# Value products with the weights as the moving operand: two heads on different column halves, output already turned

## The reference

```
p = softmax(q k^T * scale + bias)           # A; B: p1 - lam * p2; C: exp(log weights); D: with a sink
o = einsum('hqk,khd->qhd', p, v)            # 256 queries x 64 per head, causal
branch = o.reshape(256, 256) @ w_br[b]      # 256 x 1024, times sigmoid(h @ w_gate[b]), summed over b
```

## Time and profile before

| | |
|---|---|
| median of 3 runs | 709.2 us (707.84 to 709.97) |
| the profiled execution | 708.31 us, of which the span is 706.5 us |
| TensorE busy | 681.2 us, 96% of the span |
| VectorE, ScalarE busy | 246.4 us, 192.7 us |
| DMA | 243.57 MB, mean 345 GB/s |
| granted TensorE clock | 0.992 of 2.4 GHz over the span |

### The profile page before, as it was taken

How to read it: one execution, slowest core, us unless ns; L and a number is a source line. 1 busy time by engine, 2 the same in 40 slices (tenths; PEclk the granted TensorE clock), 3 DMA queues, 4 the chain that set the end, 5 groups by cost and what they waited for, 6 DMA issues and landing times.

```text
span 706.5 us, 9936 instructions
## 1 busy us (share of the span) xinstructions
PE 681.2 (96%) x4047; PEld 398.2 (56%) x4047; DVE 246.4 (35%) x528; ACT 192.7 (27%) x305; POOL 5.2 (1%) x9
## 2 busy tenths in 40 slices
PE   9999999999999999999999999999989898998995
PEld 6999887777777864344344344344344343453433
DVE  7563566667677772121121121121121010210212
ACT  6443565588565421110110010010010010100113
POOL 0000000000000000000000000000000000000000
PEclk9999999999999999999999999999999999999998
DMA  8897741383659959999999999999999999999994
GB/s 311 290 274 232 280 138 54 106 298 119 179 160 384 397 250 376 418 428 426 425 428 427 424 428 426 429 427 426 429 429 428 429 429 424 429 423 428 417 397 169
DMA packets 47053, 243.57 MB, mean 345 GB/s; under 512 B 10352, under 2 KB 13608, under 8 KB 33704
## 3 DMA queue, kind: packets, MB, share of 16 engines
q1 hardware_dynamic: 46568, 241.45, 85.7%
q0 software_dynamic: 448, 1.59, 0.7%
HBM read 241.96 MB, written 1.07 MB: 344 GB/s over the span
## 4 chain that ended last, share of the span: by engine, by line
PE 73%; DMA 17%; DVE 5%; ACT 2%; issue 2%; POOLq 0%; SPq 0%; DVEq 0%; ACTq 0%
PE bank L1759 25%; DMA unit<-in_w 17%; PE bank L1822 10%; PE bank L1434 7%; PE bank L1435 7%; PE bank L1436 7%; PE bank L1737 4%; PE bank L1836 2%; DVE low L340 2%; PE bank L1837 1%; PE bank L1416 1%; PE bank L1796 1%; PE bank L1769 1%; ACT prob L679 1%; PE bank L1661 1%
## 5 line engine op out<-in xcount | busy, mean ns | idle before, releaser
L1759 PE MATMUL bank<-unit,xT 128*64 128x512 f32 x1024 | 229.7, 601 | 11.4 <-DMA unit<-in_w 10.4
L1759 PEld LDWEIGHTS bank<-unit,xT 128*64 128x64 f32 x1024 | 75.8, 138 | 150.2 <-issue 144.5
L1822 PE MATMUL bank<-unit,hidT 128*64 128x512 f32 x480 | 106.3, 595 | 0.0
L1434 PE MATMUL bank<-high,hT_hi 128*128 128x512 f32 (+2 forms) x208 | 79.7, 383 | 1.6 <-DVE low L340 1.1
L1435 PE MATMUL bank<-low,hT_hi 128*128 128x512 f32 (+2 forms) x208 | 77.4, 372 | 0.0
L340 DVE TENSOR_TENSOR low<-unit,high 128x2048 fp32r<-128x2048 f32 (+1 forms) x34 | 70.7, 2098 | 10.3 <-ACT high L335 10.2
L1822 PEld LDWEIGHTS bank<-unit,hidT 128*64 128x64 f32 x480 | 33.1, 137 | 61.5 <-issue 60.0
L1436 PE MATMUL bank<-high,hT_lo 128*128 128x512 f32 (+2 forms) x176 | 65.1, 370 | 0.0
L335 ACT ACTIVATE high<-unit 128x2048 fp32r<-128x2048 f32 (+1 forms) x34 | 59.1, 1758 | 14.6 <-DMA unit<-in_w_in 12.0
L1311 DVE TENSOR_TENSOR y_lo<-bank,y_hi 128x512 fp32r<-128x512 f32 x30 | 20.8, 692 | 94.1 <-ACT y_hi L823 94.1
L1737 PEld LDWEIGHTS bank<-pick,hk 128*128 128x128 bf16 x768 | 44.4, 98 | 13.5 <-issue 12.2
(11 more groups left out here) (253 smaller groups left out, 681.4 us busy)
## 6 DMA issues: line engine op xcount, KB each, us to landing
unit<-in_w SPq DMA_DIRECT2D x80, 2048.0 KB, 30.4
unit<-in_w SPq DMA_DIRECT2D x24, 1024.0 KB, 10.9
unit<-in_w_gate SPq DMA_DIRECT2D x8, 2048.0 KB, 9.9
unit<-in_w SPq DMA_DIRECT2D x12, 512.0 KB, 15.8
unit<-in_w_in SPq DMA_DIRECT2D x2, 2048.0 KB, 18.0
unit<-in_w_o SPq DMA_DIRECT2D x2, 2048.0 KB, 10.6
unit<-in_w_in SPq DMA_DIRECT2D x6, 512.0 KB, 7.6
unit<-in_w_in SPq DMA_DIRECT2D x3, 1024.0 KB, 12.1
```

What stands on the lines that cost most here:

```text
L1434: mm(dst, a_hi, b_hi, start=first, stop=False)
L1759: last = mm(bank[4 + w][g * CAP:(g + 1) * CAP, :], xT[:, k, g * CAP:(g + 1) * CAP], rhs, start=(k == 0), stop=(k == KD - 1))
L1822: last = mm(bank[6 + n][g * CAP:(g + 1) * CAP, :], hidT[:, c, g * CAP:(g + 1) * CAP], rhs[:, c, n * BANK:(n + 1) * BANK], start=(c == 0), ...
```

## The change

For A, C and D the value product is turned round: `vv` (128 keys x 64) is the stationary operand and the turned weights `pT` (keys x 256 queries, then keys x 128 queries) the moving one. It is done for two heads at once in the odd steps, the even head on output partitions 0 to 63 and the odd head on 64 to 127, so that the result is `oT` itself. `turn`, `head_output` and `o` stay for B alone. There are two `pT` buffers. The softmax division of A and D moves ahead of the transposes: `weights_of_head(ahead)` on VectorE scales `prob` (128x128 and 128x256), and `middle` waits for that in place of the exponentials. The turned outputs are in bank 3 (A, C, first half of D) and bank 0 (second half of D).

```diff
-        pT = place("pT", [P, MAP])
+        pT0 = place("pT0", [P, MAP])
...
+        pT1 = place("pT1", [P, MAP], offset=shared + 7168)
...
+            if b == D_:
+                return bank[(3, 0)[c]][:, 0:TOK]
+            return bank[7 if b == B_ else 3][:, c * TOK:(c + 1) * TOK]
...
+        def values_done(st):
+
+            b, h = divmod(st, 4)
+            return (0, 2, 6, 8)[b] + (h + 1 if b == B_ else (h + 1) // 2)
...
             def keys_on_rows(st):
 
-                if st >= 1:
-                    act.wait_ge(s["pv"], st)
+                read_by = st - 1 if st // 4 == B_ else st - 1 - st % 2
+                if read_by >= 0:
+                    act.wait_ge(s["pv"], values_done(read_by))
+                pT = turned_weights(st)
...
             def turned_high(b, c=1):
-                act.wait_ge(s["oTps"], halves_turned(b, c))
+                if b == B_:
+                    act.wait_ge(s["oTps"], 1)
+                else:
+                    act.wait_ge(s["pv"], values_done(4 * b + 2 * c + 1))
...
+            def weights_of_head(st):
+
+                par = st % 2
+                if st // 4 == D_:
+                    dve.wait_ge(s["maps"], st - 3)
+                    link(nc.vector.tensor_tensor(lsum[:, par, 0, :], lsum[:, par, 0, :], esink[:, par, :], ALU.add))
+                else:
+                    dve.wait_ge(s["maps"], st + 1)
+                link(nc.vector.reciprocal(lsum[:, par, 0, :], lsum[:, par, 0, :]))
+                for t, (c0, c1) in enumerate(TILE_COLS):
+                    last = nc.vector.tensor_scalar(prob[par][:, 0, c0:c1], prob[par][:, 0, c0:c1], lsum[:, par, 0, t:t + 1],
+                                                   None, ALU.mult)
+                last.then_inc(s["probs"], 1)
...
             front(0)
+            weights_of_head(0)
             for st in range(16):
...
                 if ahead and ahead // 4 == B_:
                     difference(ahead)
+                elif ahead and ahead // 4 != C_BR:
+                    weights_of_head(ahead)
...
-                head_output(st)
+                if b == B_:
+                    head_output(st)
...
+            def values_of_two(st):
+
+                b, h = divmod(st, 4)
+                pe.wait_ge(s["pt"], st + 1)
+                if b == C_BR:
+                    pe.wait_ge(s["oev"], 4)
+                elif b == D_:
+                    pe.wait_ge(*((s["sread"], 16) if h == 3 else (s["oTs"], halves_turned(C_BR, 1))))
+                for keys in range(NT):
+                    dst = turned_part(b, h // 2)[:, keys * P:]
+                    cols = slice(0, TOK) if keys == 0 else slice(TOK, MAP)
+                    for head in (st - 1, st):
+                        c = V_AT[b] + (D_HEADS[head % 4] // 2 if b == D_ else head % 4) * HD
+                        rows = slice((head % 2) * HD, (head % 2) * HD + HD)
+                        last = mm(dst[rows, :], vv[:, keys, c:c + HD], turned_weights(head)[:, cols],
+                                  start=(keys == 0), stop=(keys == NT - 1), skip_group_check=True)
+                last.then_inc(s["pv"], 1)
...
-                else:
-                    turn(D_, [0])
...
-                if b in (B_, D_) and h == 0:
-                    turn(b - 1)
                 gate_half(st, 1)
                 if b == C_BR and h == 0:
 
-                    turn(1)
-                values(st)
+                    turn_heads()
+                if b == B_:
+                    values(st)
+                elif h % 2:
+                    values_of_two(st)
...
             branch(D_, 0, [0])
-            turn(D_, [1])
             branch(D_, 1, [0])
```

More of the change, by code:

```diff
@@ L398, in turned_part, with turned_rows, turned_weights @@
         def turned_part(b, c):
-            return bank[c][:, 0:TOK] if b == D_ else bank[7][:, c * TOK:(c + 1) * TOK]
+            if b == D_:
+                return bank[(3, 0)[c]][:, 0:TOK]
+            return bank[7 if b == B_ else 3][:, c * TOK:(c + 1) * TOK]
+        def turned_rows(b):
+            return bank[7 if b == B_ else 3][:]
+        def values_done(st):
+            b, h = divmod(st, 4)
+            return (0, 2, 6, 8)[b] + (h + 1 if b == B_ else (h + 1) // 2)
+        def turned_weights(st):
+            return pT1 if st % 2 and st // 4 != B_ else pT0
         def halves_turned(b, c):
@@ L460, in load_expert_unit @@
                     else:
-                        sp.wait_ge(s["pv"], 16)
+                        sp.wait_ge(s["pv"], values_done(15))
                 else:
@@ L700, in turned_high @@
                 else:
-                    nc.scalar.activation(oT_hi[:].rearrange("p c t -> p (c t)"), bank[7][:], ACT.Copy).then_inc(s["oTh"], 1)
+                    nc.scalar.activation(oT_hi[:].rearrange("p c t -> p (c t)"), turned_rows(b), ACT.Copy).then_inc(s["oTh"], 1)
             exponentials(0)
@@ L1027, in head_output @@
             def head_output(st):
[L1029 to L1039, removed]
-                else:
-                    dve.wait_ge(s["pv"], st + 1)
-                    last = nc.vector.tensor_copy(o[:, :, h * HD:(h + 1) * HD],
-                                                 bank[3][:, 0:P].rearrange("p (t d) -> p t d", t=NT))
-                last.then_inc(s["oev"], 1)
+                h = st % 4
+                dve.wait_ge(s["pv"], values_done(st))
+                nc.vector.tensor_copy(o[:, :, h * HD:(h + 1) * HD],
+                                      bank[3][:, 0:P].rearrange("p (t d) -> p t d", t=NT)).then_inc(s["oev"], 1)
             heads = o[:].rearrange("p t (h d) -> p (t h) d", d=HD)
@@ L1067, in turned @@
                 else:
-                    nc.vector.tensor_tensor(oT_lo[:].rearrange("p c t -> p (c t)"), bank[7][:],
+                    nc.vector.tensor_tensor(oT_lo[:].rearrange("p c t -> p (c t)"), turned_rows(b),
                                             oT_hi[:].bitcast(F32).rearrange("p c t -> p (c t)"),
@@ L1588, in values, with turn_heads @@
                 mm(bank[3][:, HD:2 * HD], pT[:, TOK:MAP], vv[:, 1, c:c + HD], start=False, stop=True).then_inc(s["pv"], 1)
-            def turn(b, halves=range(2)):
-                if b == B_:
-                    pe.wait_ge(s["ob"], 1)
-                pe.wait_ge(s["oev"], 4 * b + 2 * halves[-1] + 2)
-                if b == D_:
-                    pe.wait_ge(s["sread"], 16)
-                elif b >= 1:
-                    pe.wait_ge(s["mrg"], 4 * b)
-                for c in halves:
+            def values_of_two(st):
[14 more added lines that the diff above has]
+                last.then_inc(s["pv"], 1)
+            def turn_heads():
+                pe.wait_ge(s["ob"], 1)
+                pe.wait_ge(s["mrg"], 4)
+                for c in range(2):
                     for t in range(NT):
-                        last = nc.tensor.transpose(turned_part(b, c)[:, t * P:(t + 1) * P], o[:, t, c * P:(c + 1) * P], ident)
+                        last = nc.tensor.transpose(turned_part(B_, c)[:, t * P:(t + 1) * P], o[:, t, c * P:(c + 1) * P], ident)
                 last.then_inc(s["oTps"], 1)
```

18 lines of the change are left out of this document (10 added, 8 removed).

## The result

The changed kernel takes 710.11 us (median of 20 runs, 709.33 to 711.07) against 709.12 us (20 runs, 707.84 to 710.05). The ratio is 1.0016, with a 95% interval of 1.001 to 1.0022: 1.0 us up, where 1.7 us down was forecast. The time lies inside the range given and on the other side of no change.

A forecast was written before the change was run, and what follows sets the result against it. The prediction took the last third as bound by the expert-weight stream, started by TensorE's entry into the experts; step-by-step shifts in attention summed to -1.7 us, 709.2 to 707.5 us, range 704.9 to 710.5.

The forecast's parts named there:

- The price of the new form: Turned value product of two heads (values_of_two): 0.98 us for a pair in place of 1.34.
- less one beat: Sign for the pair's price: 0.9 to 1.05 us from the gate's last product to the branch's second, one beat subtracted.
- The lower bound: Lower estimate of a pair's price from the last experts' products, with 0.07 us per load: 0.90 us.
- The rival with the halves in turn: Column halves run one after the other: 1.47 us a pair, +1.2 us in all, 710.4 us; chance 0.12.
- The wait in step 0: TensorE waits 0.3 us before middle in step 0, for the softmax scaling on VectorE.
- The hidden savings: Rival: savings behind the chains of steps 4, 8 and 12 come out too, -3.8 us, 705.4 us; chance 0.19.
- The idle time of 0.6 to 1 us in front of the branch products: Sign: in steps 8 and 12 TensorE idles that long before the branch product, until oT_lo releases it.
- Step 4: the turn goes, and it was cover only. ... Now -0.62: Attention step 4: branch product waits for oT_lo, whose chain comes 0.2 us earlier; running shift -0.62 us.
- oT_lo comes 0.9 + 1.2 us after 214.51's place, just covered: Behind step 15: TensorE's work covers the wait for oT_lo, 2.37 us in place of 2.84, -0.47 us.
- `merge` starts at about 207.1, where it did: VectorE in step 14: the added weight scaling leaves the start of merge unmoved, at about 207.1.
- the two signs of being wrong: Middle waiting for the scaling in every head of A and D, or merge and low parts running later than now.
- So whatever moves TensorE's entry into the experts moves the stream and the end by as much: TensorE's expert entry starts the weight stream, so the end shifts equally, up to DMA's 4 us and more idle time.

The follow-up runs named there:

- e12: Changed kernel with both heads of a pair written to the lower column half; 1.65 us for a pair, total 2796.45 us on the program's spare path.
- e3: Changed kernel with the first value product of branch B (step 4) in bank 7 in place of bank 3; 709.00 us, ratio 1.0002.
- e11: Kernel before with its warming stretch in 151 short pieces, 256 instructions more ahead of the expert loop; 709.12 us, ratio 1.0001.
- e13: Kernel before with TensorE's loop over the expert pairs written out, no jump back; 712.77 us, ratio 1.0054.
- e10: Kernel before with its warming stretch in 98 short pieces, 150 instructions more ahead of the expert loop; 710.28 us, ratio 1.0015.
- e5: Changed kernel with 41 products and their loads added to the warming stretch, restoring the expert loop's old place; 708.47 us, ratio 0.9996.
- e6: Changed kernel with step 4's values in bank 7 and 42 products with loads added to the warming stretch; 707.43 us, ratio 0.9981.
- e14: Changed kernel with step 4's values in bank 7 and TensorE's expert loop written out, no padding; 709.09 us, ratio 1.0005.
- e7: Changed kernel with the loops of values_of_two exchanged, both key blocks of one head before the other head's; 709.62 us, ratio 1.0010.

## Why the prediction was wrong, point by point

**The price of the new form was right.** A pair costs 1.00 us where I took 0.98. (The sign that I gave for it, "less one beat", should have said two, since the count began at the gate's last product; less one beat it would be 1.23.) The lower bound used 0.07 us for a load, which misread its row: a load takes 0.14 (136 ns on average in the last pair), and two lie side by side in that time. Of the edges, 0.09 and 0.10 us are the slower starts before and behind it (0.32 and 0.33 for 0.23). The Trainium skill says that changing the tiling mode drains TensorE (TensorEngine Tiling (Array Packing), Key Properties). The first edge is the only trace of it here, if it is that; the second was 0.32 already before, behind `values` without any tiling. The rival with the halves in turn was priced at 1.47 for a pair, and e12, which forces it, measures 1.65; its condition didn't hold in the changed kernel.

**The wait in step 0** was right in place and size: 0.35 for 0.3 us.

**The hidden savings** of steps 8 and 12 stay hidden, as the chain through `oT_lo` said, and the gates of steps 12 and 14 (184.19 to 185.07, 202.01 to 203.18) stay where the chain sets them: 3.87 us behind the branch products before, 3.86 and 3.87 after. The idle time of 0.6 to 1 us in front of the branch products, which I had named as a sign, was not met. In step 8 it is 2.16, since the wait in front of `values` has merged into it, and in step 12 it is 0.42, with 0.58 in front of the gate.

**The first failed step is "Step 4: the turn goes, and it was cover only. ... Now -0.62".** The diff adds `pe.wait_ge(s["oTs"], halves_turned(A_, 1))` to `values` of B's first head, since bank 3 now holds A's turned outputs until `oT_lo` has read them. Before, these values ran while the chain to `oT_lo` was under way, and only the branch product waited. Now their 0.66 us lie behind that chain: 112.69 to 113.35. I had listed the chain, and not what the new wait puts behind it. Size: 0.78 us on the timeline (-0.62 forecast, +0.16 found). e3 takes this one wait away and gets 0.63 us of it back in the rows. Its median is 1.6 us lower, with intervals of some 0.7 us on each, and includes how many executions of each had the slow stretch behind step 8; the rows are the better size.

**A smaller step of the same kind is the last stretch, "oT_lo comes 0.9 + 1.2 us after 214.51's place, just covered".** From the last pair to the last branch product I forecast 2.37 us and the trace has 2.60. Timeline of ScalarE and VectorE there:

```profile
214.83 0.87 PE L1635 MATMUL bank<-pT,vv 128*64 128x256 f32 x8
215.21 0.69 DVE L1109 TENSOR_TENSOR hk<-hk,sig 128x512 f32<-128x512 f32 x1
216.00 0.60 ACT L756 ACTIVATE sig<-bank 128x512 f32<-128x512 f32 x1 [3.02 <-DVE hk L1109]
216.49 0.38 ACT L720 ACTIVATE oT_hi<-bank 128x256 fp32r<-128x256 f32 x1
...
216.90 0.42 DVE L1088 TENSOR_TENSOR oT_lo<-bank,oT_hi 128x256 fp32r<-128x256 f32 x1 [1.00 <-ACT oT_hi L720]
```

The turned outputs are there at about 215.7, but the high part stands on ScalarE behind the sigmoid of the merge (L756), which waits for `hk` until 215.90. I had counted only what the pair itself takes. What makes `hk` late begins in step 14, with another reading that failed, "`merge` starts at about 207.1, where it did". The timeline of VectorE there:

```profile
206.24 2.29 DVE L1131 TENSOR_TENSOR br_low<-unit,br_high 128x2048 fp32r<-128x2048 f32 x1
208.44 0.68 DVE L1103 SCALAR_TENSOR_TENSOR sig<-sig,bank 128x512 f32<-128x512 f32 x1
```

`weights_of_head(15)` stands in front of the low part of `w_br` and waits for its exponentials until 205.4. So `merge` starts at 208.44, less 0.74 that is 207.70, 0.5 us later than before, and without the spare 0.90 us; the next `hk` ends 0.5 us late too. That `merge` would run later was one of the two signs of being wrong that I had named. No run takes this wait away. These 0.23 us and the 0.78 of step 4 are the missing 1.05, but for 0.04.

**The second is "So whatever moves TensorE's entry into the experts moves the stream and the end by as much".** The entry came 0.54 us earlier and the final stores 1.45 us later (both less 0.74). I had put the stretch behind the attention stage down as "not changed". The text of the program isn't, but its place in the packets of code is. TensorE's compiled program had 7,117 instructions and has 7,035, all of the 82 missing ahead of the loop. The loop is 1,667 instructions, 6.5 packets of 256 instructions of 64 bytes. That the packets carry TensorE's code their number over the whole span shows: 27 before, 28 in e11 with 256 instructions more, 34 in e13 with 1,613 more. Depending on where it begins the loop touches 7 packets or 8. No trace shows where the borders lie, but one placing of them fits all nine rows of the table: with 7 the second pass runs from what is already there, with 8 the code is fetched a second time (nine packets more). The borders repeat after 256 instructions, and at +256 the old picture is back (e11). The kernel before lay on the good side by less than 30 instructions, which is luck of this kernel and nothing that the change was about. Size: 1.7 us between the two groups of the table. In medians, e10 against e11, the same program apart from its warming pieces, 1.16 us; e5 against the changed kernel by their ratios, 0.0020, 1.4 us.

**The sum again.** Forecast -1.7. The wait in step 4 adds 0.8, the last stretch 0.2, another 0.1 comes between the last branch product and the first expert product (44.23 us for 44.11, not explained), and the code adds 1.7 (1.2 to 1.4 in medians). Together that is +1.1, or +0.6 to +0.8 with the code by medians; +1.0 was measured, interval 0.7 to 1.6. With both repaired, e6 stands at -1.4 us in medians, which the forecast's -1.7 meets within the interval, and at -1.2 in rows.

**What stays open.** The nine code packets more are only 0.15 MB, 0.35 us of the stream; but 0.41 MB of weights are missing after, 0.44 in e10, 0.35 in e14 for 7 packets more. So a packet of 16 KB goes with some 0.05 MB of weights held back, about three times its size. And 0.41 MB are 0.96 us of the 1.7; where the rest goes is open. That the packets and not the stop are the cost is shown by e14 and e13; by what mechanism each takes that much is not.

## What to carry to other kernels

When a diff gives a buffer a second use, ask for every new wait what was running under the chain that it waits for: work that was cover becomes work behind. When an edit changes the number of instructions of an engine with a long loop, compare the code packets of the stage of the loop first; if they came up, put as many instructions back ahead of it, and judge the edit only then. A kernel that is bound by DMA pays for code too. And where medians are 1 us apart with intervals as wide, measure between two marks in the trace on either side of the question: here the distance from the first expert product to the final stores separates the two groups by 1.7 us and scatters by 0.4 and 0.7 within them.

## What the runs showed of the hardware

- Code comes in packets of 16 KB through the same DMA engines as the data. A loop of 1,667 instructions of TensorE is fetched again in its second pass or not, depending on its place modulo 256 instructions: at 0, +1, +60 and +256 against the kernel before it isn't, at -83, -82, -34, -30 and +150 it is, with stops of 2.3 to 3.5 us at and behind the jump back. All nine fit a border between 7 and 8 packets touched.
- Beside a stream of 427 GB/s, six to nine code packets more between 440 and 640 us cost 1.7 us (440.3 to 440.7 against 441.8 to 442.5 us), whether TensorE stops for 6.3 us or not at all.
- Behind 2.17 us without a product in step 8 of e3 the granted clock fell to the lower level (0.51 in the window from 150.5 to 154 us); behind 2.16 us in the changed kernel it stayed at 1.00.
- Two float32 products on the two column halves run at once although the program issues the whole of one head first: 1.01 us for a pair in e7, 1.00 with the halves in turn, 1.65 on one half in e12. The Trainium skill (TensorE: Matmul & The Clock Gate, The mechanism) has products start and end strictly in program order, and weight loads overlap running products only if the row group differs (a sentence before, it also names a background weight buffer). By the first a pair in e7's order could overlap only where the program passes from one head to the other, and would come near the 1.65 us of e12. For column halves the times of e7 disagree with the first. e12 disagrees with the second: its eight loads of 0.14 us each, outside the products, would bring 1.1 us on top of the 1.3 expected for the products, and the pair takes 1.65.
